# Sixteen small copies of each hidden block: issued by GpSimd in place of ScalarE

## The reference, cut to what matters

```python
def _swiglu(h, w_gate, w_up, w_down):
    return (jax.nn.silu(h @ w_gate) * (h @ w_up)) @ w_down
...
    for l in range(DEPTH):
        ada = (jax.nn.silu(c) @ w_ada[l] + b_ada[l]).reshape(b, N_ADA, 1, D_MODEL)
        h = _modulate(_rmsnorm(x, g_ffn1[l]), sh1, sc1)
        x = x + 0.5 * gt1 * _swiglu(h, w1_gate[l], w1_up[l], w1_down[l])
        h = _modulate(_rmsnorm(x, g_mix[l]), sh2, sc2)
        x = x + gt2 * _token_mix(h, w_in[l], w_out[l])
        h = _modulate(_rmsnorm(x, g_ffn2[l]), sh3, sc3)
        x = x + 0.5 * gt3 * _swiglu(h, w2_gate[l], w2_up[l], w2_down[l])
    return _rmsnorm(x, g_final)
```

## Time and profile before

| | |
|---|---|
| median of 3 runs | 1866.02 us |
| the profiled execution | 1864.46 us |
| its span, first to last instruction | 1862.7 us |
| outside the span | 1.8 us |
| PE busy | 1839.9 us (99%) |
| DVE busy | 1333.1 us (72%) |
| ACT busy | 1002.7 us (54%) |
| POOL busy | 0.2 us |
| granted TensorE clock, mean | 0.999 |

### The profile page before, as it was taken

One profiled execution on the slowest core, in us unless ns is written; L12 is line 12 of the kernel. 1 busy time (PEld: TensorE's weight loads), 2 busy tenths in 40 slices (PEclk: granted clock), 3 DMA queues, 4 the chain that ended last, 5 costly groups with the idle time before them and its releaser, 6 DMA issues.

```text
span 1862.7 us, 21446 instructions
## 1 busy us (share of the span) xinstructions
PE 1839.9 (99%) x8260; PEld 1525.1 (82%) x8260; DVE 1333.1 (72%) x1388; ACT 1002.7 (54%) x1343; POOL 0.2 (0%) x4
## 2 busy tenths in 40 slices
PE   7999999999999999999999999999999999999998
PEld 6888888888888888888888888888888888888887
DVE  7998988878888887776655777677755554555565
ACT  6556776434565644645544456555555335655544
POOL 0000000000000000000000000000000000000000
PEclk9999999999999999999999999999999999999999
DMA  9998899998898997685354565777665555556554
GB/s 392 415 415 335 340 347 369 390 360 342 341 351 345 361 347 277 260 327 214 136 186 153 204 241 210 271 283 283 262 219 193 193 190 196 192 193 216 198 192 141
DMA packets 118470, 506.64 MB, mean 272 GB/s; under 512 B 13792, under 2 KB 14048, under 8 KB 99040
## 3 DMA queue, kind: packets, MB, share of 16 engines
q1 hardware_dynamic: 118080, 504.94, 73.0%
q10 hardware_dynamic: 288, 0.33, 0.1%
HBM read 503.10 MB, written 2.12 MB: 271 GB/s over the span
## 4 chain that ended last, share of the span: by engine, by line
PE 94%; ACT 2%; DVE 2%; DMA 1%; issue 1%; SPq 0%; ACTq 0%; DVEq 0%
PE banks L1206 31%; PE banks L1208 31%; PE banks L1207 31%; DMA w_raw<-w_chunks 1%; DVE scratch L925 1%; ACT w_hi L675 1%; ACT scratch L705 0%; DVE w_lo L913 0%; DMA residual<-x_t 0%; PE banks L1253 0%; PE banks L1266 0%; ACT scratch L788 0%; PE banks L1277 0%; PE banks L1305 0%; PE banks L1294 0%
## 5 line engine op out<-in xcount | busy, mean ns | idle before, releaser
L675 ACT CAST w_hi<-w_raw 128x1024 fp32r<-128x1024 f32 x652 | 684.3, 1052 | 797.3 <-PE banks L1208 693.8
L913 DVE TENSOR_TENSOR w_lo<-w_raw,w_hi 128x1024 fp32r<-128x1024 f32 x652 | 791.4, 1221 | 415.3 <-ACT w_hi L675 414.3
L1206 PE MATMUL banks<-w_hi,x_split 128*128 128x512 f32 x1776 | 697.8, 393 | 2.7 <-DVE x_split L1057 1.0
L1208 PE MATMUL banks<-w_hi,x_split 128*128 128x512 f32 x1776 | 691.7, 389 | 0.0
L1207 PE MATMUL banks<-w_lo,x_split 128*128 128x512 f32 x1776 | 691.1, 389 | 0.0
L1206 PEld LDWEIGHTS banks<-w_hi,x_split 128*128 128x128 f32 x1776 | 333.6, 188 | 72.4 <-issue 2.6
L1208 PEld LDWEIGHTS banks<-w_hi,x_split 128*128 128x128 f32 x1776 | 333.4, 188 | 70.1
L1207 PEld LDWEIGHTS banks<-w_lo,x_split 128*128 128x128 f32 x1776 | 333.7, 188 | 67.6
L1206 PE MATMUL banks<-w_hi,hidden 128*128 128x512 f32 (+1 forms) x712 | 275.4, 387 | 0.0
L1207 PE MATMUL banks<-w_lo,hidden 128*128 128x512 f32 (+1 forms) x712 | 275.3, 387 | 0.0
L1208 PE MATMUL banks<-w_hi,hidden 128*128 128x512 f32 (+1 forms) x712 | 275.3, 387 | 0.0
(11 more groups left out here) (142 smaller groups left out, 649.6 us busy)
## 6 DMA issues: line engine op xcount, KB each, us to landing
w_raw<-w_chunks SPq DMA_DIRECT2D x656, 512.0 KB, 4.2
ada_raw<-w_ada_tiles SPq DMA_DIRECT2D x102, 1024.0 KB, 7.1
ada_early<-w_ada_tiles SPq DMA_DIRECT2D x32, 1024.0 KB, 9.0
ada_raw_low<-w_ada_tiles SPq DMA_DIRECT2D x10, 1024.0 KB, 6.0
gate_row<-gate_rows SPq DMA_DIRECT2D x3, 1024.0 KB, 6.8
residual<-x_t SPq DMA_DIRECT2D x2, 1024.0 KB, 7.9
out_t<-residual SPq DMA_DIRECT2D x7, 256.0 KB, 2.4
table<-tables SPq DMA_DIRECT2D x1, 1664.0 KB, 11.2
```

What stands on the lines that cost most here:

```text
L675: nc.scalar.copy(w_parts(c)[0], raw[:, c % RING, :]).then_inc(hi_ready, 1)
L913: nc.vector.tensor_tensor(lo, raw[:, c % RING, :], hi.bitcast(F32), ALU.subtract).then_inc(lo_ready, 1)
L1206: nc.tensor.matmul(o, x_hi, hi, start=(first and k == k0), stop=False, skip_group_check=True)
L1208: ins = nc.tensor.matmul(o, x_lo, hi, start=False, stop=(last and k == k0 + KC - 1), skip_group_check=True)
```

## The change

ACT loses `move_hid`. GpSimd gets a program of its own that does the same sixteen copies for each body in one run, with no place in the table: for each body it waits for the turn of that body (`hid_turned`) and for the `hid_lo` of the body before (`hid_ready`, since that frees `s3`), copies, and counts `hid_moved`. `hid_hi` and `hid_lo` stand at 6 and 7 chunk numbers behind the turn, where they stood at 4 and 5 or more; turns stand at least 7 apart, where it was 6 (and moves at least 9 apart). So the turns of bodies 1, 2 and 3 move from 57, 63, 69 to 58, 65, 72; their `hid_hi` from 64, 73, 82 to 64, 71, 78; that of body 5 from 100 to 101; body 4's from 91 to 89; for body 0 and for bodies 6 to 21 two numbers later than before.

```diff
-TURN_AT, MOVE_AT = [], []
+TURN_AT = []
 for g in GROUPS:
     if g.kind == UP:
-        TURN_AT.append(max([g.last] + [c + 6 for c in TURN_AT[-1:]]))
-        MOVE_AT.append(max([TURN_AT[-1] + 1] + [c + 9 for c in MOVE_AT[-1:]]))
+        TURN_AT.append(max([g.last] + [c + 7 for c in TURN_AT[-1:]]))
...
             put(TURN_AT[g.n], ("turn_hid", g.n))
-            for r in range(4):
-                put(MOVE_AT[g.n] + r, ("move_hid", (g.n, r)))
-            put(MOVE_AT[g.n] + 3, ("hid_hi", g.n))
-            put(MOVE_AT[g.n] + 4, ("hid_lo", g.n))
+            put(TURN_AT[g.n] + 6, ("hid_hi", g.n))
+            put(TURN_AT[g.n] + 7, ("hid_lo", g.n))
...
-            def move_hid(b, r):
-
-                if r == 0:
-                    act.wait_ge(hid_turned, b + 1)
-                    if b > 0:
-                        act.wait_ge(hid_ready, b)
-                for q in range(4):
-                    ins = nc.scalar.copy(s3[32 * r:32 * r + 32, q * T:q * T + T],
-                                         hid_plain[32 * q:32 * q + 32, hid_at(b), 0, r * T:r * T + T])
-                if r == 3:
-                    ins.then_inc(hid_moved, 1)
...
+        @block.gpsimd
+        def _(pool):
+            for b in range(2 * BODIES):
+                pool.wait_ge(hid_turned, b + 1)
+                if b > 0:
+                    pool.wait_ge(hid_ready, b)
+                for r in range(4):
+                    for q in range(4):
+                        ins = nc.gpsimd.tensor_copy(s3[32 * r:32 * r + 32, q * T:q * T + T],
+                                                    hid_plain[32 * q:32 * q + 32, hid_at(b), 0, r * T:r * T + T])
+                ins.then_inc(hid_moved, 1)
```

More of the change, by code:

```diff
@@ L846, in ret_hi @@
                 nc.scalar.copy(y_pair(p)[0], by_tile(y_bank(p), 2)).then_inc(y_hi, 1)
-            stage = {"silu": silu, "restore": restore, "move_hid": lambda m: move_hid(*m), "hid_hi": hid_high, "in_keep": in_keep, "squares": squares, "root": take_root,
+            stage = {"silu": silu, "restore": restore, "hid_hi": hid_high, "in_keep": in_keep, "squares": squares, "root": take_root,
                      "tail_squares": tail_squares, "warm_root": warm_root, "final": final, "mod": modulate, "turn_qk": keep_qk, "exp": exp, "turn_p": keep_p, "split_att": att_hi,
```

## The result

The changed kernel takes 1881.91 us (median of 4 runs, 1880.30 to 1883.63) beside 1865.45 us for the kernel before: ratio 1.009, interval 1.0078 to 1.0102, so 16.5 us slower. The forecast was 17.9 us slower. The size was right, and that was largely luck: the time is lost in other places and by another mechanism than the sum had, as the rest shows.

A forecast was written before the change was run, and what follows sets the result against it. PE was taken as the bound. 18.9 us of PE lateness from DVE exclusion less 1.0 us won at the restore gave +17.9 us on the 1866.0 us median: 1883.9 us, range 1863.5 to 1914.

The forecast's parts named there:

- What bounds the kernel: PE, busy 1839.9 of 1862.7 us; taking the copies off ACT wins only a 1.0 us restore wait.
- Part 2, the limit: In the last body POOL has 14.9 us from the turn's end until ACT reaches `hid_hi`.
- Part 3, a copy's price: One 32x256 copy on POOL was taken as 0.42 us, sixteen as 6.7 us.
- Part 4, who is stopped: POOL's copies and DVE's `w_lo` and `w_ada` steps exclude each other, each copy paid in DVE time: 40.3 us, bodies 0 to 5.
- its share of the sum, 18.9 us: PE's lateness at about 300 us: 40.3 less 17.0 DVE idle, 3.7 for products, 0.75 lead of `w_lo`.
- rival B: Not slower: DVE isn't held, or so briefly that idle time swallows it; 14.9 us limit kept: 1865.0 us, chance 0.33.
- waits of ACT at `hid_hi` as a sign: ACT's waits at `hid_hi` for POOL should show in bodies 0 to 10 and not in 11 to 21.
- signs named beforehand: Profile after: wider copy spacing in bodies 0 to 5, longer `w_lo` and `w_ada`, PE waiting 15 to 20 us for `w_lo`.
- sign of failure: The forecast fails if copy spacing is under 0.22 or over 0.6 us, DVE isn't held, or its idle is less usable.
- Bodies 6 to 10 and the down product: Bodies 6 to 10 pay nothing, 4.4 us over against 5.9 lead; body 5's down product, 2.7 us less spare, counted nothing.
- Late loads: In 170 to 322 us late DVE steps make late SP loads; costed at nothing, some us more if that fails.
- The clock: The granted clock should stay at 1.00, since no pause is long.

The follow-up runs named there:

- experiment 7: The changed kernel with each GpSimd copy replaced by a GpSimd memset of the same 32x256: 1864.46 us, 0.9997 of the kernel before.
- experiment 1: The kernel before, its copies left on ACT, plus 96 useless GpSimd copies of 32x256 in bodies 0 to 5: 1865.65 us, 1.0003.
- experiment 6: The changed kernel with the copies of body 10 alone back on ACT: 1877.41 us, 1.0065 of the kernel before.
- experiment 2: The kernel before, its copies left on ACT, plus 96 useless GpSimd copies of 512 columns in bodies 0 to 5: 1874.78 us, 1.0054.

## Why the prediction was right, and where it wasn't

**What bounds the kernel**: right. PE is the bound, and ACT's relief is worth at most 2.4 us by experiment 7; the forecast had 1.0.

**Part 2, the limit**: right in form, wrong in that it was read in one body. The last body has 14.9 us, and 14.8 came. In the full stretch DVE comes to its turns later, behind `w_lo` and `w_ada` steps, and body 1 had 11.7 us. And the limit was never set against POOL's pace in the early bodies: "one body: 6.7 us of copies and five `w_lo`" was worked out for the late ones alone, where it gave 12.8 and 11.8 us came. The same working for bodies 0 to 10, with a DVE step per copy, would have given 16 steps of 1.2 to 2.35 us, well over 15 us. That is the step that failed, although the prediction named waits of ACT at `hid_hi` as a sign to look for in bodies 0 to 10: it expected them and gave them no price. They came in ten of these eleven bodies (not in body 2), and against the prediction in 11, 13 and 14 too, 2.4 to 2.6 us each.

**Part 3, a copy's price**: right, 0.42 taken and 0.435 measured.

**Part 4, who is stopped**: the exclusion is real, and the steps said to be hit are those that are hit, but the two sides don't pay alike. The prediction's "one waits for the other to end" fits POOL's copy; DVE's step grew by only 0.13 to 0.19 us of the copy's 0.40, and the measurement decides. 40.3 us were put on DVE, 9.9 came; its share of the sum, 18.9 us, is 0.8 us by experiment 1. What POOL pays, from 1.3 to 2.4 us for a copy, wasn't in the sum at all. So rival B had the better premise, a hold so brief that idle time swallows it; its forecast failed because it took the limit to be kept with ease, which is the same step. Of the signs named beforehand, copies spaced wider in bodies 0 to 5 and `w_lo` steps longer than 1.22 us came true; PE's wait for `w_lo` of 15 to 20 us didn't, it is 2.7. And one sign of failure was met: a spacing over 0.6 us, for sixteen copies in 19.2 us are 1.2 us apart.

**Bodies 6 to 10 and the down product**: wrong. The prediction saw that `hid_lo` has less spare before the down product and counted nothing. It cost 3.4 us of pause and 1.7 of slow clock in the trace; experiment 6, which took it away, came out 4.5 us lower.

**Late loads**: wrong, by little. They were costed at nothing; the 1.5 us at chunks 107 to 114 stand behind them.

**The clock**: wrong. "No pause is long" was said; one of 7.5 us, and one of 3.5 us, each brought a stretch at the lower level, 3.9 us in all.

So a term of 18.9 us that measured 0.8 and a set of pauses of 17 us that wasn't foreseen happened to be of one size. That the number came out is luck. Less luck is in the sign: the full stretch of DVE at 170 to 322 us does hold 10.5 of the 17.8 us, but they are lost through POOL's lateness, and 5.1 more at body 10, where nothing was expected. What stays open: the 0.7 us at chunk 6, which lies ahead of the first copy and shows in several kernels of this study, wasn't looked into; the chains at chunks 94 and 107 to 114 are argued from the trace; and POOL's turn-taking is read from starts and ends, while what grants a turn isn't seen.

## What to carry to other kernels

When work goes to an engine that shares something with a full one, cost the guest's slowness first: ask how long its run of instructions takes if each waits for a whole instruction of the host, and who stands in order at the semaphore behind it. A wait put into an engine's fixed order costs what is queued behind it; so count what PE wants next behind each such wait, and look at the tightest stretch, not at the easiest body. A loss that comes from missed limits isn't proportional: half of the copies, or two bodies moved with more room for the others, took all of it away.

## What the runs showed of the hardware

- A GpSimd copy that reads SBUF and a DVE instruction with two SBUF inputs take turns, instruction by instruction. The GpSimd copy of 32x256 goes from 0.40 us to as long as the DVE step, up to 2.37 us; the DVE step grows by 0.13 to 0.19 us for 256 columns and 0.35 to 0.40 us for 512. That is less than the copies' own 0.40 and 0.61 us, and near what 256 more columns add to a copy that nothing holds: the shortest take 0.390 us for 256 and 0.605 for 512, so 0.21.
- Beside DVE steps with one SBUF input neither is held: in the run of experiment 2 the 13 copies of 512 columns that ran inside a product or a turn took 0.61 us, and these DVE steps kept their 1.21 and 1.25 us.
- A GpSimd memset of the same size isn't held (305 ns in the stretch of 170 to 322 us, 0.25 us apart) and doesn't lengthen DVE's steps.
- After a pause of 7.5 us PE ran 5 us at a clock of 0.51; after one of 3.5 us, a shorter while (0.61 over 675 to 679 us):

```profile
675.00:679.00 4.00, 4.00 (x12) 3.14 (x13) 4.00 (x3) 0.39 (x1) 0.00 (x0) 0.61 0.55 190
```
